# A hybrid streaming-encoder block on one core: the experts' gather of token rows is issued one block further ahead

## The chip, the cores and the metric

One core of one Trainium2 chip runs the whole layer in one launch. The metric is the device time of the program in microseconds; the median of several runs is compared.

## What is computed

The reference is one layer over 2048 tokens of width 1024: a mixing part (sparse attention and an mLSTM, each projected, gated and added to the residual), and then a mixture of experts. Only the experts matter here:

```
y = zeros(t, dm)
buf_tok, block_e = tokens sorted by expert, each expert padded to whole blocks of 128
xb = xn[buf_tok].reshape(nblk, 128, 1024)
def expert_block(xblk, e):
    hid = silu(xblk @ w_gate[e]) * (xblk @ w_up[e])      # 1024 -> 512, twice
    return hid @ w_down[e]                                # 512 -> 1024
y[buf_tok] += expert_block(...) * gate weight
```

There are 32 experts, each token goes to two of them, and the reference works in float32. With these inputs the padded list has 48 blocks of 128 rows; the table has room for 63.

## The kernel before

The stages follow one another: norm and input projection, indexer and top-k, attention and mLSTM, output projection with the router, and last `route_and_experts`, which the change touches. That function first sorts the tokens: it makes a table of row indices `IX` (one column of 128 indices for each block), the expert of each block `BE`, and the number of blocks in use, `used` (48 here). Then it runs the blocks, and last it combines: for each tile of tokens the two rows of results are gathered and added to the residual.

Float32 products are made as three products of rounded halves: each weight tile and each activation tile is split into a high part (a cast on ScalarE) and a low part (a subtraction on VectorE). A block `n` goes through these steps, each engine with its own program and semaphores between them:

- SyncE's queue loads the weights of a block into `raw`, one buffer deep: 8 pairs of gate and up tiles (`load_gate_up`, lines 575 and 576, 256 KB each) as soon as the low part of the tile that was there is made, then 4 down tiles (`load_down`, line 583, 512 KB each). A load whose expert is the one already there is skipped.
- GpSimd gathers the block's 128 token rows of 4 KB (`gather`, line 638) into one half of the tile `XG`, from a column of indices that it copies first (`indices`, line 641). The same engine stores each block's result (`store`, line 648) after ScalarE and VectorE have copied it out of PSUM into `Y`, each one half (lines 786 and 923).
- TensorE transposes the rows (`rows_t`, line 700, into `e_pX`), multiplies by gate and up (`gate_up`, line 710, 48 matmuls into `e_pG`), transposes the hidden values (line 717, `e_pH`) and multiplies by down (`down`, line 728, 24 matmuls into `e_pY`).
- ScalarE makes the high parts (`e_x_hi` line 761, `e_h_hi` 778, weights 768 and 781) and the Silu (773); VectorE makes the low parts (901, 915, weights 906 and 918) and the product of gate and up (911).

TensorE is software-pipelined. Its turn `n` of the loop is: transpose the hidden values of block n-1, gate and up of block n, the rows of block n+1, down of block n-1. So the transposes of block n+1 stand behind the gate-and-up matmuls of block n. GpSimd's turn `n` waits until gather n has landed (`x_in`) and until the rows of block n-1 are transposed (`xt_ps`), which frees the half of `XG` that gather n+1 writes; it copies the indices of block n+1, gathers block n+1, and then waits for the result of block n-1 and stores it. Each engine's program is run in order, and there is one store and one gather in each turn. A gather also sits in the same software queue of DMAs as the stores.

The final gather of the loop is one past the last block in use (its rows are transposed, but no product uses them).

Of the kernel before, what the change touches and what calls it, by code (L numbers as in the profile page):

```python
# [11 lines left out]
I32 = mybir.dt.int32  # L12
# [5 lines left out]
P = 128  # L18
# [22 lines left out]
NBLK = 63  # L41
# [64 lines left out]
def hold(eng, held):  # L106

    eng.sem_inc(held, 1)


def identity(nc, pool, tile, sem):

    nc.gpsimd.memset(tile, 0.0).then_inc(sem, 1)
    pool.wait_ge(sem, 1)
    nc.gpsimd.affine_select(out=tile, in_=tile, compare_op=ALU.not_equal, fill=1.0, base=0,
                            pattern=[[-1, P]], channel_multiplier=1).then_inc(sem, 1)
# [374 lines left out]
def route_and_experts(pg, LG, BI):  # L491
# [5 lines left out]
    with ExitStack() as c:  # L497
        sb = lambda n, s, d=F32: c.enter_context(nc.sbuf_tensor("e_" + n, s, d))
        sem = pg.semaphores(c, "e_", "y_ps ya_ok yv_ok")
        raw = sb("raw", [P, NU, 1024])  # L500
        w_hi, w_lo = sb("w_hi", [P, NU, 1024], F32R), sb("w_lo", [P, NU, 1024], F32R)
        IX, IXF = sb("ix", [P, NBLK + 1], I32), sb("ix_f", [P, NBLK])
        XG, ix = sb("xg", [P, 2, DM]), sb("ix_now", [P, 2], I32)
        x_hi, x_lo = sb("x_hi", [P, KT, P], F32R), sb("x_lo", [P, KT, P], F32R)
        SG, H = sb("sg", [P, DE]), sb("h", [P, DE])
# [51 lines left out]
        x_in, y_st = pg.sw_sem("e_x_in"), pg.sw_sem("e_y_st", primed=True)  # L557
# [3 lines left out]
        def blocks_in_use(eng):  # L561

            eng.wait_ge(be_ok, 1)
            return (eng.value_load(BE[0:1, USED:USED + 1], min_val=2 * NT, max_val=NBLK),
                    eng.value_load(BE[0:1, LAST:LAST + 1], min_val=2 * NT - 1, max_val=NBLK - 1))
# [51 lines left out]
        @block.gpsimd  # L617
        def _(pool):
            g = nc.gpsimd
            g.iota(w4i[:, 0, :], [[-1, NG]], base=NG, channel_multiplier=0)  # L620
            g.iota(w8i[:, 0, :], [[-1, EG]], base=EG, channel_multiplier=0)
            g.iota(ti[:, :, :], [[0, 2], [1, NT]], base=0, channel_multiplier=0)
            g.iota(pi[:, :], [[0, 1]], base=0, channel_multiplier=1)
            g.iota(ci[:, :], [[1, P]], base=0, channel_multiplier=0).then_inc(r_set, 1)
            g.memset(ones[:, :], 1.0)
            g.memset(IX[:, NBLK:NBLK + 1], 0)
            g.memset(lt[:, :], 1.0).then_inc(r_set, 1)
            pool.wait_ge(r_set, 2)
            g.affine_select(out=lt[:, :], in_=lt[:, :], compare_op=ALU.is_gt, fill=0.0, base=0,
                            pattern=[[1, P]], channel_multiplier=-1).then_inc(r_set, 1)  # L630
            identity(nc, pool, IDN[:, :], setup)
            g.memset(Z[:, :], 0.0).then_inc(setup, 1)
            pool.wait_ge(hot_ok, 1)
            g.tensor_tensor(in_blk[:, :, 1, :], hot, tf[:, :, :].broadcast_to([P, 2 * NT, NBLK]), ALU.mult).then_inc(blk_ok, 1)
            used, end = blocks_in_use(pool)

            def gather(n, b):
                pool.indirect_dma_start(XG[:, b, :], None, pg.d["xn"], bass.IndirectOffsetOnAxis(ix[:, b:b + 1].bitcast(U32), 0)).then_inc(x_in, 16)

            def indices(n, b):  # L640
                nc.gpsimd.tensor_copy(ix[:, b:b + 1], IX[:, bass.ds(n, 1)]).then_inc(ix_ok, 1)  # L641
                pool.wait_ge(ix_ok, n + 1)
                hold(pool, held)

            def store(n):
                pool.wait_ge(ya_ok, n + 1 + START)
                pool.wait_ge(yv_ok, n + 1 + START)
                pool.dma_start(yb_d[bass.ds(n * P, P), :], Y[:, :]).then_inc(y_st, 16)
            pool.wait_ge(tab_ok, 1)
            indices(0, 0)  # L650
            gather(0, 0)
            indices(1, 1)
            pool.wait_ge(x_in, 16)
            gather(1, 1)
            with pool.Fori(0, NBLK // 2) as t:
                for b in range(2):
                    n = 2 * t + b + 1
                    with pool.If(n < used):
                        pool.wait_ge(x_in, 16 * n + 16)
                        pool.wait_ge(xt_ps, n)  # L660
                        indices(n + 1, b)
                        gather(n + 1, b)
                        store(n - 1)
            store(end)
            pool.wait_ge(x_in, 16 * used + 16)
            pool.wait_ge(y_st, 16 * used + PRIMED)
            hold(pool, held)
            pool.wait_ge(gl, KT * used + KT)
            hold(pool, held)
            for t in range(NT):  # L670
                if t >= YBUF:
                    pool.wait_ge(c_ok, t - YBUF + 1)
                for k in range(2):
                    pool.indirect_dma_start(YG[t % YBUF][:, k, :], None, yb_d, bass.IndirectOffsetOnAxis(SL[:, k, t:t + 1].bitcast(U32), 0)  # L674
                                            ).then_inc(g_in[t % YBUF], 16)
# [1755 lines left out]
def build(nc, ins, out):  # L2431
    pg = Prog(nc, ins)
    pg.out = out
    with ExitStack() as c:
        h_hi = c.enter_context(nc.sbuf_tensor("h_hi", [P, KT, SEQ], F32R))
        h_lo = c.enter_context(nc.sbuf_tensor("h_lo", [P, KT, SEQ], F32R))
        project_head(pg, h_hi, h_lo)
        tail_and_index(pg, h_hi, h_lo)
    attend_and_recur(pg)
    with ExitStack() as c:  # L2440
        LG, BI = c.enter_context(nc.sbuf_tensor("logits", [P, NT, NG + NE], F32)), c.enter_context(nc.sbuf_tensor("router_bias", [P, 1, NG + NE], F32))
        merge_and_output(pg, LG, BI)
        route_and_experts(pg, LG, BI)
# [15 lines left out]
```

## Time and profile before

| | |
|---|---|
| median of 3 runs | 3496.93 us (3492.85 to 3497.88) |
| the profiled execution's own time | 3494.54 us |
| its span | 3492.5 us |
| TensorE busy | 3015.0 us (86% of the span) |
| VectorE busy | 2485.5 us (71%) |
| ScalarE busy | 1836.7 us (53%) |
| GpSimd busy | 449.1 us (13%) |
| mean granted TensorE clock | 0.936 |
| DMA, mean over the span | 154 GB/s |

The busy times are shares of the whole span, over stages with different limits. What bounds the expert stage is read from that stage: from the order of the instructions on each engine, with the idle time before each and what ended it. In the rows below PE is TensorE, PEld its weight loads, DVE VectorE, ACT ScalarE, POOL GpSimd, SPq the DMA queue of SyncE. `e_xg` is the tile XG, `e_ix_now` the copied indices, `slot_out` the results in memory. L with a number is a line of the kernel.

### The profile page before, as it was taken

What the parts mean: (1) busy time and instruction counts of PE and PEld (TensorE: products, weight loads), DVE (VectorE), ACT (ScalarE), POOL (GpSimd) and SP (SyncE); (2) the same over time, 40 slices, a digit from 0 to 9 for tenths busy, and PEclk for the clock granted to TensorE, in tenths of its full rate; (3) what the DMA queues carried; (4) which work ended last, traced back from release to release, by engine and by line L of the source; (5) the groups of instructions that cost most, each with busy time, mean ns of one, the idle gap of its engine ahead of it and who ended that gap; (6) DMA issues with size and microseconds to landing.
All of it is one profiled execution on the core that took longest, in us unless ns stands there. A gap on an engine that the chain in (4) does not pass through costs nothing. (4 is left out here: it accounts for less than half of the span.)

```text
span 3492.5 us, 45322 instructions
## 1 busy us (share of the span) xinstructions
PE 3015.0 (86%) x12983; PEld 2239.0 (64%) x12984; DVE 2485.5 (71%) x3902; ACT 1836.7 (53%) x2533; POOL 449.1 (13%) x587
## 2 busy tenths in 40 slices
PE   2898599889999967999999589998599999999980
PEld 2676477668778834555545367786477777777760
DVE  4457689889989966776663344442899989898874
ACT  6232257568578633434434233332477777777760
POOL 0111100000000032221111000000111111111113
PEclk6999799999999978999999789998699999999995
DMA  3122322222212265444323455553479779666868
GB/s 108 57 76 67 101 78 77 67 70 73 77 59 74 70 150 139 114 106 116 93 59 68 127 181 167 165 175 107 159 270 338 284 285 350 246 224 255 309 267 342
DMA packets 367694, 536.98 MB, mean 154 GB/s; under 512 B 35632, under 2 KB 201040, under 8 KB 367424
## 3 DMA queue, kind: packets, MB, share of 16 engines
q1 hardware_dynamic: 338288, 430.70, 39.0%
q0 software_dynamic: 26960, 96.13, 7.4%
q10 hardware_dynamic: 2304, 8.39, 0.6%
q8 instruction: 72, 1.18, 0.1%
q14 instruction: 70, 0.57, 0.1%
HBM read 510.18 MB, written 129.80 MB: 183 GB/s over the span
## 5 line engine op out<-in xcount | busy, mean ns | idle before, releaser
L906 DVE TENSOR_TENSOR e_w_lo<-e_raw,e_w_hi 128x1024 fp32r<-128x1024 f32 x386 | 446.9, 1218 | 3.3 <-ACT e_w_hi L768 3.3
L1539 PE MATMUL x_ps<-h_hi,x_w_hi 128*128 128x512 f32 (+1 forms) x1024 | 402.2, 393 | 0.0
L1539 PE MATMUL x_ps<-h_lo,x_w_hi 128*128 128x512 f32 (+1 forms) x1024 | 400.9, 391 | 0.0
L1539 PE MATMUL x_ps<-h_hi,x_w_lo 128*128 128x512 f32 (+1 forms) x1024 | 400.5, 391 | 0.0
L768 ACT CAST e_w_hi<-e_raw 128x1024 fp32r<-128x1024 f32 x386 | 376.8, 1051 | 5.3 <-PE e_pG L710 5.3
L1729 DVE TENSOR_SCALAR_CACHE_REDUCE x_relu<-x_score,x_cand 128x1024 uint8<-128x1024 f32 (+3 forms) x217 | 315.6, 1487 | 3.6
L1642 ACT ACTIVATE x_relu<-x_score,x_cand 128x896 int8<-128x896 f32 (+3 forms) x217 | 281.0, 1296 | 55.8 <-DVE x_cand L1736 55.5
L2297 DVE CUSTOM_DVE_ANT_0 t_junk<-t_L,t_mask 128x512 bf16<-128x512 f32 (+3 forms) x320 | 185.7, 607 | 164.6 <-PE t_L L2079 163.6
L2118 PE MATMUL t_O<-t_probT,t_v 128*65 128x512 f32 x544 | 289.6, 614 | 11.8 <-ACT t_probT L2269 10.5
L2269 ACT ACTIVATE t_probT<-t_ST 128x512 f32<-128x512 f32 x272 | 160.8, 593 | 260.3 <-PE t_ST L2110 259.6
L710 PE MATMUL e_pG<-e_w_hi,e_x_hi 128*128 128x512 f32 x768 | 247.0, 402 | 3.6 <-DVE e_x_lo L901 3.6
L710 PE MATMUL e_pG<-e_w_hi,e_x_lo 128*128 128x512 f32 x768 | 242.8, 397 | 0.0
L710 PE MATMUL e_pG<-e_w_lo,e_x_hi 128*128 128x512 f32 x768 | 242.8, 397 | 0.0
L2079 PE MATMUL t_L<-t_k,t_q 128*128 128x512 f32 (+3 forms) x320 | 194.8, 658 | 43.2 <-DVE t_max_part L2297 24.8
L918 DVE TENSOR_TENSOR e_w_lo<-e_raw,e_w_hi 128x1024 fp32r<-128x1024 f32 x192 | 222.3, 1220 | 11.8 <-ACT e_w_hi L781 11.8
L1539 PEld LDWEIGHTS x_ps<-h_hi,x_w_lo 128*128 128x128 f32 (+1 forms) x1024 | 191.2, 187 | 43.2
L1539 PEld LDWEIGHTS x_ps<-h_hi,x_w_hi 128*128 128x128 f32 (+1 forms) x1024 | 191.2, 187 | 42.4
L1539 PEld LDWEIGHTS x_ps<-h_lo,x_w_hi 128*128 128x128 f32 (+1 forms) x1024 | 191.3, 187 | 40.4
L781 ACT CAST e_w_hi<-e_raw 128x1024 fp32r<-128x1024 f32 x192 | 187.1, 1057 | 0.0
L1696 DVE SCALAR_TENSOR_TENSOR x_score<-x_relu,x_iw,x_score 128x1024 f32<-128x1024 f32 (+7 forms) x154 | 152.8, 1022 | 31.3 <-ACT x_relu L1616 26.9
L1616 ACT ACTIVATE x_relu<-x_z 128x1024 f32<-128x1024 f32 (+7 forms) x176 | 139.0, 817 | 67.2 <-DVE x_score L1696 43.9
L710 PEld LDWEIGHTS e_pG<-e_w_lo,e_x_hi 128*128 128x128 f32 x768 | 145.1, 189 | 35.0
(402 smaller groups left out, 6242.9 us busy)
## 6 DMA issues: line engine op xcount, KB each, us to landing
e_raw<-in_w_exp_gate SPq DMA_DIRECT2D x392, 256.0 KB
e_raw<-in_w_exp_up SPq DMA_DIRECT2D x392, 256.0 KB
e_raw<-in_w_exp_down SPq DMA_DIRECT2D x192, 512.0 KB
projT<-x_out SPq DMA_DIRECT2D x124, 256.0 KB
slot_out<-e_y POOLq DMA_DIRECT2D x48, 512.0 KB, 6.1
o_gate<-projT SPq DMA_DIRECT2D x32, 512.0 KB
x_w_raw<-in_w_in SPq DMA_DIRECT2D x31, 512.0 KB
x_t<-in_x SPq DMA_DIRECT2D x16, 512.0 KB
```

What stands on the lines that cost most here:

```text
L710: last = nc.tensor.matmul(psG[:, q, :], x[:, k, :], w[:, k, q * DE:(q + 1) * DE], start=(k == 0 and r == 0), stop=(k == KT - 1 and r == 2))
L768: nc.scalar.copy(w_hi[:, u, :], raw[:, u, :]).then_inc(gh, 1)
L781: nc.scalar.copy(w_hi[:, KT + k, :], raw[:, KT + k, :]).then_inc(dh, 1)
L906: nc.vector.tensor_tensor(w_lo[:, u, :], raw[:, u, :], w_hi[:, u, :].bitcast(F32), ALU.subtract).then_inc(gl, 1)
L918: nc.vector.tensor_tensor(w_lo[:, KT + k, :], raw[:, KT + k, :], w_hi[:, KT + k, :].bitcast(F32), ALU.subtract).then_inc(dl, 1)
L1539: last = nc.tensor.matmul(ps[0:w, u % 4, :], wt[:, m % 2, kk, 0:w], ht[:, kk, q * 512:(q + 1) * 512], start=(kk == 0 and s == 0), stop=(kk ...
L1642: nc.scalar.activation(unused[j][:, 0:width(n)], S[:, j, 0:width(n)], ACT.Sign, bias=cand[:, j:j + 1].bitcast(F32), accum_out=cnt[:, j:j + ...
L1729: last = v.tensor_scalar(unused[j][:, 0:width(n)], S[:, j, 0:width(n)], cand[:, j:j + 1].bitcast(F32), 0.0, ALU.is_ge, ALU.add, accum_out= ...
L2079: nc.tensor.matmul(L[:, made % 3, 0:hi - lo], Q[:, n % 4, h, :], KS[:, v, lo:hi], start=True, stop=True).then_inc(l_ok, 1)
L2118: nc.tensor.matmul(O[0:AD + 1, :, :], V[:, j, v, :], PT[:, (FIRST[s] + j) % 3, :], start=(j == 0), stop=(j == n)).then_inc(pv_ok, 1)
L2269: a.activation(PT[:, f % 3, :], ST[:, u % 2, :], ACT.Exp).then_inc(p_ok, 1)
L2297: v_.tensor_tensor_reduce(junk[:, seen % 3, 0:hi - lo], L[:, seen % 3, 0:hi - lo], MB[:, n % 4, lo:hi], 1.0, -3e38, ALU.add, ALU.max, mxp[ ...
```

## The change

The index table gets one more column, set to zero like the one before it. Before the loop GpSimd now issues the gather of block 2 as well, after gather 1 has landed and block 0 has been transposed. Turn `n` of the loop then waits for gather n+1 and for the transposes of block n, and gathers block n+2 into the other half of XG, ahead of the store of block n-1. The last wait counts one gather more.

```diff
-        IX, IXF = sb("ix", [P, NBLK + 1], I32), sb("ix_f", [P, NBLK])
+        IX, IXF = sb("ix", [P, NBLK + 2], I32), sb("ix_f", [P, NBLK])
...
-            g.memset(IX[:, NBLK:NBLK + 1], 0)
+            g.memset(IX[:, NBLK:NBLK + 2], 0)
...
             indices(1, 1)
             pool.wait_ge(x_in, 16)
             gather(1, 1)
+            pool.wait_ge(x_in, 32)
+            pool.wait_ge(xt_ps, 1)
+            indices(2, 0)
+            gather(2, 0)
             with pool.Fori(0, NBLK // 2) as t:
                 for b in range(2):
                     n = 2 * t + b + 1
                     with pool.If(n < used):
-                        pool.wait_ge(x_in, 16 * n + 16)
-                        pool.wait_ge(xt_ps, n)
-                        indices(n + 1, b)
-                        gather(n + 1, b)
+                        pool.wait_ge(x_in, 16 * n + 32)
+                        pool.wait_ge(xt_ps, n + 1)
+                        indices(n + 2, 1 - b)
+                        gather(n + 2, 1 - b)
                         store(n - 1)
             store(end)
-            pool.wait_ge(x_in, 16 * used + 16)
+            pool.wait_ge(x_in, 16 * used + 32)
```

## Rows read from the trace of the kernel before

**Rows 1.** The page's 40 slices of the span: TensorE's granted clock in tenths.
```profile
PEclk6999799999999978999999789998699999999995
```

**Rows 2.** View by window, first store to last but one: us, busy, clock, DMA share, GB/s.
```profile
2528.82:3390.65 861.83, 837.76 (x3855) 674.16 (x3853) 776.06 (x736) 645.87 (x735) 134.58 (x139) 1.00 0.76 282
```

**Rows 3.** Order of time on POOL: start us, us, instruction, idle before it and releaser.
```profile
2528.82 0.59 POOL L648 DMA_DIRECT2D slot_out<-e_y  x1 [34.60 <-DVE e_y L923]
...
2604.50 0.58 POOL L648 DMA_DIRECT2D slot_out<-e_y  x1 [15.94 <-DVE e_y L923]
2605.08 1.21 POOL L641 COPY e_ix_now<-e_ix 128x1 int32 x1
2607.08 1.16 POOL L638 DMA_INDIRECT e_xg<-xn,e_ix_now  x1 [0.79 <-POOL e_ix_now L641]
2622.60 0.58 POOL L648 DMA_DIRECT2D slot_out<-e_y  x1 [14.36 <-DVE e_y L923]
...
2642.18 0.58 POOL L648 DMA_DIRECT2D slot_out<-e_y  x1 [15.83 <-DVE e_y L923]
...
3390.65 0.58 POOL L648 DMA_DIRECT2D slot_out<-e_y  x1 [16.15 <-DVE e_y L923]
```

**Rows 4.** Order of time on PE, around the transposes of two blocks.
```profile
2614.39 1.04 PE L700 MATMUL e_pX<-e_ident,e_xg 128*128 128x128 f32 x8
...
2632.03 0.63 PE L710 MATMUL e_pG<-e_w_hi,e_x_lo 128*128 128x512 f32 x2
2633.90 1.09 PE L700 MATMUL e_pX<-e_ident,e_xg 128*128 128x128 f32 x8 [1.24 <-DMA e_xg<-xn,e_ix_now]
```

**Rows 5.** Chain of waits, same stretch: start us, us, what.
```profile
2625.18 8.68 DMA e_xg<-xn,e_ix_now
```

**Rows 6.** Waits from 2528.82 to 3390.65: us in total, times, longest.
```profile
PE e_pX L700 <- DMA e_xg<-xn,e_ix_now: 21.8, 24, 1.6
PEld e_pX L700 <- DMA e_xg<-xn,e_ix_now: 36.1, 31, 2.0
SPq L108 <- DVE e_w_lo L918: 183.9, 184, 3.6
```

**Rows 7.** The gathers of token rows, from issue to landing.
```profile
DMA to landing us min/median/max: 4.4/7.6/9.0
```

**Rows 8.** Order of time on POOL, PE, SP's queue and ACT at the first blocks.
```profile
2493.06 1.16 POOL L638 DMA_INDIRECT e_xg<-xn,e_ix_now  x1 [0.79 <-POOL e_ix_now L641]
2504.25 1.04 PE L700 MATMUL e_pX<-e_ident,e_xg 128*128 128x128 f32 x8
2510.70 0.38 SPq L576 DMA_DIRECT2D e_raw<-in_w_exp_up  x1
2516.57 1.05 ACT L768 CAST e_w_hi<-e_raw 128x1024 fp32r<-128x1024 f32 x1 [0.28 <-PE e_pG L710]
```

**Rows 9.** View by window, the two of 50 us with the highest DMA share.
```profile
2650.00:2700.00 50.00, 49.53 (x231) 39.92 (x230) 45.38 (x44) 36.97 (x44) 7.58 (x9) 1.00 0.98 367
2900.00:2950.00 50.00, 49.78 (x228) 39.64 (x227) 45.17 (x44) 38.73 (x45) 8.76 (x9) 1.00 1.04 399
```

**Rows 10.** DVE: one copy of a result (order of time), and all waits before it.
```profile
2621.17 0.69 DVE L923 COPY e_y<-e_pY 128x512 f32<-128x512 f32 x1 [0.70 <-PE e_pY L728]
DVE e_y L923 <- PE e_pY L728: 43.6, 46, 1.1
```

**Rows 11.** Loads on SP's queue, the cast behind them, and landings of 512 KB there.
```profile
2613.16 0.08 SPq L575 DMA_DIRECT2D e_raw<-in_w_exp_gate  x1
2650.82 0.35 SPq L575 DMA_DIRECT2D e_raw<-in_w_exp_gate  x1
2663.50 5.79 ACT L768 CAST e_w_hi<-e_raw 128x1024 fp32r<-128x1024 f32 x6
DMA to landing us min/median/max: 5.5/8.3/10.5
```

**Rows 12.** Chain of waits: the gate-and-up matmuls of block 0 and of block 8.
```profile
2491.15 13.26 PE e_pG L710 x48
2641.04 11.19 PE e_pG L710 x48
```

## The prediction

> **What bounds the kernel now.** I read the page first. The change touches only the expert stage, which runs from about 2477 us to 3411 us; TensorE's clock stands at its full level there except at the two ends [rows 1]. A view by window from the first store of a block to the store of the last block but one says how tight it is [rows 2]: 861.83 us, PE busy 837.76 of them, VectorE 776.06, ScalarE 645.87, the DMA engines at 0.76. TensorE sets the pace, and what it lacks is some 24 us. Next I read GpSimd's order of time [rows 3]. Each block shows a store, a copy of indices and a gather, and the distance between two stores is the period of a block: 18.10 us from 2604.50 to 2622.60, 19.58 from there to 2642.18. From the first store to the last one listed are 46 periods. I counted them in that view: 15 are 18.09 to 18.12 us and 31 are longer (18.33 to 19.88). Then TensorE's order of time [rows 4]: in the short period the transposes of a block's token rows (e_pX) follow the gate-and-up matmuls without a gap; in the long one they start at 2633.90, though the matmuls before them were issued to the end by 2632.5. The chain of waits gives the reason [rows 5]: the gather issued at 2625.18 lands 8.68 us later, at 2633.86, and the transposes start 0.04 us after that. The waits of the stretch say the same in sum [rows 6]: PE and its weight loads wait before e_pX for the gather and for nothing else. Both lines see the same gaps, so they are not added.
>
> The arithmetic of one gather: it is issued 2.58 us behind the store (2607.08 against 2604.50), which waits for the result of the block two before. The transposes want it at 2614.39, 7.31 us after its issue. Gathers take 4.4 to 9.0 us to land, 7.6 in the median [rows 7]. So about a third are in time and the rest cost up to 1.8 us.
>
> **The change, part by part.** The loop does the same three things in the same order, but the gather in it is for block n+2 instead of n+1. In time each slot still holds a store and, 2.58 us behind it, a gather; only whose rows it fetches is new.
> - *The gather's lead.* A slot's gather is now wanted one period later: 7.31 + 18.10 = 25.4 us after its issue, against 9.0 at the longest. No transposes should wait. All 46 periods become 18.10: 46 x 18.10 = 832.6 us instead of 861.83, **29.2 us less**. (Summed over the 31 long periods alone the excess over 18.10 is also 29.2.)
> - *Its new waits.* It waits for the gather before it (issued 18.1 us earlier, landed within 9.0) and for the transposes of block n, which frees its half of XG. In the old order of time the transposes at 2614.39 stand ahead of the store at 2622.60, behind which the new gather comes. Both are met when POOL gets there. Cost 0. Queued behind the gather is the store of block n-1, for whose result POOL waits some 14.4 us after the gather anyway. If a wait did hold POOL, it would have to do so for that long before Y, and with it the copies of the next result, came late.
> - *POOL's and the queues' load.* Per block the same copy (1.2 us), the same gather, the same store. One more gather in all, of a block past the last, and one column more set to zero long before: 0. SP's queue is not passed by anything.
> - *The start.* The gather of block 2 goes out as before, at 2493.06; the gather of block 3 moves from 2531 to some 2 us after the transposes of block 1, so to about 2507.3 [rows 8]. That falls among the loads of block 2's gate and up weights, whose last is issued at 2510.70. It adds 512 KB; at the 399 GB/s that the busiest window moved [rows 9] that is 1.3 us. ScalarE casts the late ones from 2516.57 on, waiting for PE then, and the matmuls that read them come only after the result of block 0, behind 2527. I take 0 and keep 0 to 1.3 us.
> - *What is late next.* With the gather gone, VectorE: in the short period it still waits 0.70 us for the result of the down matmuls before it copies it [rows 10], and it does that in every one of the 46. Its start is set by PE each time, so short periods in a row don't eat that margin. SP waits 183.9 us for VectorE in its queue, 4 us per block, so it isn't the bound either [rows 6]. ScalarE waits for PE alone.
> - *The weights' cover.* In a block with a new expert SP issues the first load at 2650.82 and ScalarE casts it at 2663.50, 12.7 us later. Loads of 512 KB on that queue landed in 5.5 to 10.5 us [rows 11]. That leaves 2.2 us at the worst and 4.4 in the median.
>
> Sum: 3494.54 (the profiled execution's own time) - 29.2 = 3465.3. That execution is 2.4 us under the median of the three runs, 3496.93, so the median should be **3467.7 us**.
>
> At one place a rule of the Trainium skill speaks against the change. Its page "DMA: Bandwidth & Descriptors", section "Anatomy of one DMA — SWDGE (gpsimd) path", has a DMA issued from GpSimd take 2.0 us plus its bytes at 436 GB/s; for the 512 KB of a gather that is an estimate of 3.2 us. By it every gather would be in time already, and the sum would be 0. The measured landings [rows 7] are all longer, so the rule gets no term here.
>
> **The rivals.**
> *A, the gather is not what the transposes lack, no change.* A wait is put down to the semaphore that came last, so the name could be wrong, and a gather could always be in time, as by the skill's rule above. It would give 3497. Against it: 0.04 us between landing and start, and gaps only where the landing is beyond 7.3 us. Chance 0.04.
> *B, the DMA engines hold part of the gain.* Where several experts in a row are new, the DMA engines are full: 399 GB/s at a share of 1.04 in one window of 50 us, 367 at 0.98 in another [rows 9]. Such a block moves 16 loads of 256 KB and 4 of 512 KB of weights, a gather and a store of 512 KB each, in all 7 x 1024 KB = 7.34 MB; at 399 GB/s that is 18.4 us, and the periods there are 18.33 to 18.47. If that bound them and not the gather, they would keep 0.35 us each. SP's own times tell the blocks with new weights from the others, 0.34 us for a load that runs and 0.08 for one that is skipped [rows 11]; the longest row of them is 5 blocks, so weights fall behind by 1.7 us at most, inside the cover of 2.2 to 4.4 us; hence I believe they will run at 18.1. If not, some 9 blocks keep 3.2 us (gain 26.0, 3471), and if all 31 blocks with new weights (32 experts) did, 10.9 us (gain 18.3, 3479). Chance 0.10.
> *C, slower: TensorE's clock.* Without its pauses TensorE is busy all the time, and the grant could fall from 2.4 to 1.2 GHz for stretches. Price: the gate-and-up matmuls of block 0, partly at the lower level, took 13.26 us, at the full level 11.19 [rows 12]; that is 2.07 us each time, so the gain is gone when it happens in more than 14 of the 46 blocks; in all 46 it would be 95 us lost, less 29 gained, 3563. Against it: the grant was at half where PE was idle and 1.00 over the whole stretch with PE at 97% [rows 2]. Chance 0.03.
>
> **The numbers.** The forecast has 0.83, B 0.10, A 0.04, C 0.03. The forecast's own range is 3463 to 3473 (the three runs lie 4 us below to 1 us above their median; the start may cost 1.3). With B's upper case the range is 3461 to 3478. A measurement of this kernel can tell about 0.2%, 7 us, from no change. Faster by more: forecast and B, 0.93. Within: A, 0.04. Slower: C, 0.03.
>
> **What would show it.** After the change GpSimd's stores should stand 18.1 us apart in all 46 periods, the waits before e_pX should be gone from PE and its loads, the gathers should land in the same 7 to 9 us, DMA_INDIRECT e_xg should count 50 instead of 49, and the same window should be 833 us with PE busy at 99% or more. B shows as periods of 18.4 with ScalarE waiting for a DMA before its casts, or VectorE's 0.70 us gone; A as unchanged gaps; C as a PEclk below 1.00 within the stretch. I am wrong if the stage shortens by less than 26 us.

## The result, and the profile after

The changed kernel takes 3463.52 us in the median of 4 runs (3459.86 to 3467.85) against 3497.40 us (3492.85 to 3499.34) for the kernel before, measured beside it: ratio 0.9904, 95% interval 0.9892 to 0.9917. The forecast was 3467.7 us in a range of 3461 to 3478.

The first view again by window, from the first store of a block to the store of the last block but one (us of stretch, busy time of PE, PE's loads, DVE, ACT, POOL, granted clock, DMA share, GB/s):

```profile
2530.37:3363.52 833.15, 831.58 (x3855) 677.20 (x3854) 773.91 (x736) 646.01 (x735) 132.81 (x138) 1.00 0.79 290
```

Against [rows 2] the stretch is 28.7 us shorter, with the same 3855 matmuls. PE is busy for all but 1.6 us of it, at the same full clock, and the DMA engines move about the same bytes in less time (282 GB/s over 861.83 us, 290 over 833.15). The order of time on POOL shows where the distance between two stores has gone (against [rows 3]; an edit shifts the line numbers, so L923 of the kernel before is L927 here, L700 is L704, L710 is L714 and L728 is L732):

```profile
2507.00 0.18 POOL L641 COPY e_ix_now<-e_ix 128x1 int32 x1 [10.94 <-PE e_pX L704]
2507.97 0.97 POOL L638 DMA_INDIRECT e_xg<-xn,e_ix_now  x1 [0.79 <-POOL e_ix_now L641]
2530.37 0.59 POOL L648 DMA_DIRECT2D slot_out<-e_y  x1 [21.43 <-DVE e_y L927]
...
2602.77 0.58 POOL L648 DMA_DIRECT2D slot_out<-e_y  x1 [14.38 <-DVE e_y L927]
2603.35 1.20 POOL L641 COPY e_ix_now<-e_ix 128x1 int32 x1
2605.34 1.16 POOL L638 DMA_INDIRECT e_xg<-xn,e_ix_now  x1 [0.79 <-POOL e_ix_now L641]
2620.89 0.58 POOL L648 DMA_DIRECT2D slot_out<-e_y  x1 [14.38 <-DVE e_y L927]
...
3363.52 0.58 POOL L648 DMA_DIRECT2D slot_out<-e_y  x1 [14.38 <-DVE e_y L927]
```

The gather still follows the store by 2.57 us, and 44 of the 46 periods are 18.07 to 18.13 us. The other two are 19.52 and 16.70 us, 36.22 together: one store was issued 1.4 us late, with no releaser that the profile names, and nothing behind it moved. GpSimd pauses so in the kernel before too, one turn of its loop later and ahead of a gather, which follows its store by 3.99 us instead of 2.58, in a block that had room for it (a period of 18.12 us). TensorE's order of time, at the block where it stood still before [rows 4], has no gap any more; the chain of waits of that stretch names PE alone:

```profile
2630.32 0.62 PE L714 MATMUL e_pG<-e_w_hi,e_x_lo 128*128 128x512 f32 x2
2630.78 1.03 PE L704 MATMUL e_pX<-e_ident,e_xg 128*128 128x128 f32 x8
2631.57 0.72 PE L732 MATMUL e_pY<-e_w_hi,e_h_hi 128*128 128x512 f32 x2
```

```profile
2613.70 5.61 PE e_pY L732 x24
2619.31 0.44 PE e_pH L721 x4
2619.74 11.19 PE e_pG L714 x48
2630.94 0.87 PE e_pX L704 x8
```

The landings of the gathers have not become shorter (against [rows 7]), and VectorE still waits in each of the 46 blocks for the down matmuls, 0.7 us (32.8 us in all, against [rows 10]). From the answers for the gather's line and from the waits of the stretch:

```profile
L638 POOL DMA_INDIRECT e_xg<-xn,e_ix_now x50: 967/1155/1165, 2481.3 to 3348.0; - x50
DMA to landing us min/median/max: 4.3/7.6/9.7
```

```profile
DVE e_y L927 <- PE e_pY L732: 32.8, 46, 0.7
```

The rest of the program is as it was: from the first gather's issue to the first store 49.04 us, before 48.90; from the last store of the stretch to the end of the span (3466.0 us) 102.48 us, before 101.85. The first gather itself came 1.4 us later in this execution, in stages that the change doesn't touch. So the two profiled executions differ by 26.5 us in span where the stage gives 28.7, and the medians by 33.9.

### The profile page after: what moved, and what is told of

It is laid out like the page before. It is cut to its first block and busy times, and to the rows that moved or that the text cites. A ratio compares the mean times of both kernels' runs of the same rounds, so it can differ in the third digit from the quotient of the medians.

```text
span 3466.0 us, 45327 instructions
## 1 busy us (share of the span) xinstructions
PE 3004.1 (87%) x12983; PEld 2238.1 (65%) x12984; DVE 2482.6 (72%) x3902; ACT 1836.6 (53%) x2533; POOL 447.2 (13%) x589
## 5 line engine op out<-in xcount | busy, mean ns | idle before, releaser
L714 PE MATMUL e_pG<-e_w_hi,e_x_hi 128*128 128x512 f32 x768 | 246.7, 402 | 3.6 <-DVE e_x_lo L905 3.6
L714 PE MATMUL e_pG<-e_w_lo,e_x_hi 128*128 128x512 f32 x768 | 242.6, 397 | 0.0
L714 PE MATMUL e_pG<-e_w_hi,e_x_lo 128*128 128x512 f32 x768 | 242.1, 396 | 0.0
L2083 PE MATMUL t_L<-t_k,t_q 128*128 128x512 f32 (+3 forms) x320 | 195.0, 658 | 44.1 <-DVE t_max_part L2301 26.5
L714 PEld LDWEIGHTS e_pG<-e_w_hi,e_x_lo 128*128 128x128 f32 x768 | 145.2, 189 | 35.1
```

The costliest lines, as they stand in the source:

```text
L714: last = nc.tensor.matmul(psG[:, q, :], x[:, k, :], w[:, k, q * DE:(q + 1) * DE], start=(k == 0 and r == 0), stop=(k == KT - 1 and r == 2))
L2083: nc.tensor.matmul(L[:, made % 3, 0:hi - lo], Q[:, n % 4, h, :], KS[:, v, lo:hi], start=True, stop=True).then_inc(l_ok, 1)
```

## The experiments

The theory was that only the time from a gather's issue to its use counts. The rivals were that the place in the program or the extra gather helps, that a whole block of lead is needed, that GpSimd's turn is near the path, and for the size, that there is a gain outside the stage. "The stage" below is always the stretch between the same two stores, read by window. The changed kernel, again:

> The changed kernel as it is, timed again in more rounds. The profile of after accounts for 28.7 us in the expert stage, the medians for 33.9 us. Theory (the gather's lead and nothing else): the gain settles at 27 to 31 us, ratio 0.9911 to 0.9923, and the stage from the first store to the last but one is 833 us in the profile again. Rival (the change also helps outside the stage): the gain stays at 33 to 35 us, ratio near 0.990.

It took 3464.88 us (4 runs, 3459.84 to 3469.33) beside 3495.81 us (15 runs, 3490.36 to 3500.09): 0.991, interval 0.9895 to 0.9926. The profile's stage was 833.15 us once more, to the hundredth. So the changed kernel's stage repeats; the kernel before was profiled once, 861.83 us, and the run that follows, which does the same work in the same order, has 862.84. What the medians show beyond 28.7 us (33.9, then 30.9 us) shrank in the second series and lies inside the spread of single runs: 8.0 and 9.5 us between the fastest and the slowest of the changed kernel in the two series, 6 to 18 us of the kernel before in the series measured. A gain outside the stage is not shown, and the interval doesn't exclude a few microseconds.

**The two halves of the change.**

```diff
-                        indices(n + 2, 1 - b)
-                        gather(n + 2, 1 - b)
                         store(n - 1)
+                        indices(n + 2, 1 - b)
+                        gather(n + 2, 1 - b)
```

> The changed kernel with the store of block n-1 put in front of the gather of block n+2 in the same turn. Theory (only the time between a gather's issue and its use counts, and gather n+2 behind store n-1 is what the kernel before does, written with another index): as before, 3494 to 3500 us, the stage 860 to 863 us, 30 or so long periods. Rival (being two blocks ahead in the program, with the extra gather before the loop, is what helps): as after, 3460 to 3468 us, the stage 833 us.

3494.85 us (10 runs), ratio 0.9999 (0.9987 to 1.0011), and by window:

```profile
2527.27:3390.11 862.84, 840.06 (x3855) 675.73 (x3853) 775.93 (x736) 646.16 (x735) 134.69 (x139) 1.00 0.76 282
```

The gain is gone in full. "One block further ahead" and "in front of the store" are one thing: with the store in front, the gather of n+2 waits for the result of n-1, as it did in the kernel before under another index.

**How much lead is needed.** In the kernel before, the index copy goes ahead of the store and the gather stays behind it (`hold` increments a semaphore; the index table also gets the second extra column, as in the change):

```diff
             gather(1, 1)
+            indices(2, 0)
...
                         pool.wait_ge(xt_ps, n)
-                        indices(n + 1, b)
+                        hold(pool, held)
                         gather(n + 1, b)
+                        indices(n + 2, 1 - b)
                         store(n - 1)
```

> The kernel before, gather still one block ahead and behind the store of the block before, but its indices are copied ahead of that store, so that the gather follows the store by 0.6 us instead of 2.58: some 1.9 us more lead, 9.2 us instead of 7.3. Theory (a gather that has landed is worth nothing more, so lead counts only up to the 9.0 us of the longest landing): nearly the whole gain, the stage 833 to 836 us, 3464 to 3471 us. Rival (a whole block of lead is needed, because landings stretch as the pace rises or the gather comes to lie closer behind the store's packets): landings grow to over 9.2 us, half or more of the stalls stay, 3475 to 3490 us.

3466.14 us (5 runs), ratio 0.9917 (0.9903 to 0.9931). The order of time on POOL, the stage by window, and the landings:

```profile
2600.75 0.58 POOL L648 DMA_DIRECT2D slot_out<-e_y  x1 [15.19 <-DVE e_y L925]
2601.72 1.62 POOL L638 DMA_INDIRECT e_xg<-xn,e_ix_now  x1 [0.40 <-issue]
2603.35 0.32 POOL L641 COPY e_ix_now<-e_ix 128x1 int32 x1
```

```profile
2528.35:3361.52 833.17, 831.59 (x3855) 677.12 (x3854) 773.90 (x736) 646.06 (x735) 109.53 (x138) 1.00 0.79 291
```

```profile
DMA to landing us min/median/max: 4.2/6.8/8.7
```

The gather follows the store by 0.97 to 1.26 us (2.39 once, at the pause), so 1.3 to 1.6 us sooner, not the 1.9 of the expectation, and this edit alone brings the whole gain: 833.17 us for the stage. A whole block of lead is not needed. In the changed kernel the longest landing is 9.7 us, 2.4 beyond the old lead of 7.31, so of the 18.1 us that the change adds not more than 2.4 are used.

The edit does two things, though, and the run doesn't part them: it gives lead, and it puts the gather 0.9 to 1.2 us ahead of the down loads on SP's queue, where it was 0.4 us behind them (the groups of blocks in this paragraph are told apart below, by what SP's queue loads). The landings moved both ways. In a group of 16 blocks they were 7.7 to 9.0 us and are now 6.4 to 6.9. The other 30 became longer: 15 were 7.4 to 8.2 us and are 7.9 to 8.7, and 15 were 4.7 to 5.5 us and are 5.6 to 7.1. So the rival was right that landings stretch, for 30 of the 46, and wrong in size: against a lead of some 8.6 to 8.9 us, TensorE waited once, for 0.2 us. The longest landings have next to nothing to spare.

The other way round, both kernels with the indices copied twice, which moves each gather back (in the order of time of the kernel before so edited it follows the store by 3.70 to 3.71 us, 2611 to 2671 us into the span, and by 2.58 without the edit, so by 1.13 us more and not the 2.0 of the expectations, since the second copy takes 0.97 us):

```diff
-                nc.gpsimd.tensor_copy(ix[:, b:b + 1], IX[:, bass.ds(n, 1)]).then_inc(ix_ok, 1)
-                pool.wait_ge(ix_ok, n + 1)
-                hold(pool, held)
+                for again in range(2):
+                    nc.gpsimd.tensor_copy(ix[:, b:b + 1], IX[:, bass.ds(n, 1)]).then_inc(ix_ok, 1)
+                    pool.wait_ge(ix_ok, 2 * n + again + 1)
+                    hold(pool, held)
```

> The changed kernel with the indices copied twice, so that each gather is issued about 2.0 us later. Theory: the lead falls from 25.4 to 23.4 us against landings of at most 9.7 us, no change: 3460 to 3468 us, the stage 833 us, no wait before the transposes. Rival (POOL's turn is itself near the path, so that its store or the copies behind it come late): up to 46 x 2.0 us more, over 3475 us.

The changed kernel doesn't notice: the stage 833.15 us, no wait before the transposes. Its median, 3468.48 us (4 runs, 3465.21 to 3470.20), is 0.5 us above the range expected and 3.6 above the 3464.88 us of its partner; the single runs of the two overlap, and the stage has none of it.

> The kernel before with the indices copied twice, so that each gather is issued about 2.0 us later: the lead falls from 7.3 to 5.3 us. Theory (each period is 18.10 plus what the landing takes beyond the lead): the 31 long periods grow by 2.0 us each and the 15 short ones by something under 2.0, in all 62 to 92 us: the stage 924 to 954 us, 3559 to 3589 us. Rival (the stalls are not the gather's): under 20 us more.

The kernel before does: 3531.86 us (2 runs), ratio 1.0113 (1.0083 to 1.0142), the stage 896.11 us, 34.3 more. That is half of what was expected, and in sum what the theory gives for the delay that the edit really made: 31 long periods by 1.13 us are 35.0. It holds in the sum only: single long periods changed by -0.4 to 3.8 us, since the landings moved as well, so the close agreement is in part luck. The short periods stayed short (14 of 15; one turned long, 18.70 us, at the pause of GpSimd), so those gathers had over 1.1 us to spare. The waits of the stretch:

```profile
PEld e_pX L701 <- DMA e_xg<-xn,e_ix_now: 65.9, 32, 2.8
PE e_pX L701 <- DMA e_xg<-xn,e_ix_now: 51.9, 32, 2.3
```

Two kinds of gather, then: some 30 that are late, and 15 that have room. That set the next question.

**What makes a gather late.** The kernels from here to the one with the narrow store and no loads leave out part of the stores or use wrong weights, so their results are wrong; each was executed once, and only the stage and the landings are read. First the store ahead of the gather in its queue against the loads of weights:

```diff
-                pool.dma_start(yb_d[bass.ds(n * P, P), :], Y[:, :]).then_inc(y_st, 16)
+                pool.dma_start(yb_d[bass.ds(n * P, P), 0:16], Y[:, 0:16]).then_inc(y_st, 16)
```

> The kernel before with a store of 16 of the 1024 columns in the loop (64 bytes a row instead of 4 KB); the other columns of the results are filled with zeros after the loop, so only the expert stage is to be read, and the end is longer. Theory T1 (a gather lands late because the store issued 2.58 us ahead of it fills the same software queue): landings fall by 1.3 us or more, to a median of 6.3 us or less, and the stage comes to 833 to 838 us. Theory T2 (the landing is set by the weights' loads on the other queue, or is simply what 128 rows of 4 KB take from GpSimd): the median stays at 7.3 us or more, the stage above 850 us.

The stage got longer, 870.06 us against 861.83, and the landings with it, 8.0 us in the median:

```profile
DMA to landing us min/median/max: 4.3/8.0/9.3
```

T1 fell. Why a store of 8 KB in place of 512 KB makes the gather behind it later is taken up below. Then no loads, by making all entries of the table of experts 0:

```diff
-            v.tensor_scalar(BE[:, 0:NBLK], psH[0:1, 0, 0:NBLK], float(NE - 1), None, ALU.min)
-            v.memset(BE[:, NBLK:USED], NE - 1)
+            v.tensor_scalar(BE[:, 0:NBLK], psH[0:1, 0, 0:NBLK], 0.0, None, ALU.min)
+            v.memset(BE[:, NBLK:USED], 0)
```

> The kernel before with all blocks on expert 0, so that no weights are loaded in the loop (the results use the weights of expert 0 throughout); gathers and stores are the same. T1 (the store ahead of it in the queue makes the gather late): landings stay at 7 us or more and the stage above 850 us. T2 (the weights' loads make it late): landings fall below 7.3 us nearly everywhere and the stage comes to 833 to 840 us.

```profile
2524.17:3356.71 832.54, 830.97 (x3855) 676.65 (x3853) 773.85 (x736) 646.84 (x735) 134.50 (x138) 1.00 0.18 63
```

```profile
DMA to landing us min/median/max: 4.2/4.5/7.0
```

Without loads the gather of the kernel before is in time in every block, and 832.54 us is what TensorE needs: the changed kernel is 0.6 us above it. The loads make gathers late, but not all of them alike. SP's queue in the kernel before tells which; `load_down` is issued some 0.4 us ahead of the gather at 2607.08 or 2625.18 [rows 3]:

```profile
2586.98 3.66 SPq L583 DMA_DIRECT2D e_raw<-in_w_exp_down  x4
2606.66 3.40 SPq L583 DMA_DIRECT2D e_raw<-in_w_exp_down  x4
2624.76 3.67 SPq L583 DMA_DIRECT2D e_raw<-in_w_exp_down  x4
```

A group of 3.66 or 3.67 us is one whose loads ran, one of 3.40 was skipped (its last load takes 0.07 instead of 0.34 us). Set beside the 46 periods, all 31 long periods have loads that ran, with landings of 7.4 to 9.0 us, and all 15 short ones skipped ones, with landings of 4.7 to 5.5 us. One edit each for the two kinds of loads:

```diff
-                    load_down(this, dict(cond=this != before), n - 1)
+                    load_down(this, dict(cond=this != this), n - 1)
```

> The kernel before with the down weights never reloaded in the loop (all blocks multiply by the down weights of expert 0), gate and up loads as they were. Theory T3: a gather is late where the four down loads (2 MB) are issued 0.4 us ahead of it on the other queue, as every long period of the kernel before has a down load that runs and every short one a skipped one. Then landings fall to 7.3 us or less, the stage comes to 832 to 835 us. Rival T4 (any traffic of weights does it, mostly the gate and up loads with twice the bytes): the stage stays above 845 us.

```profile
2532.14:3364.68 832.54, 830.97 (x3855) 676.68 (x3853) 773.62 (x736) 645.71 (x735) 134.38 (x139) 1.00 0.60 214
```

```profile
DMA to landing us min/median/max: 4.3/5.3/7.3
```

```diff
-                    load_gate_up(after, dict(cond=after != this), n)
+                    load_gate_up(after, dict(cond=after != after), n)
```

> The kernel before with the gate and up weights never reloaded in the loop (all blocks multiply by those of the first two experts loaded), down loads as they were. T3 (the down loads make the gather late): the same 31 or so long periods, landings up to 8.5 us, the stage 850 to 862 us. T4 (the gate and up loads do): the stage 832 to 840 us.

```profile
2534.07:3401.33 867.26, 837.54 (x3855) 674.29 (x3853) 776.41 (x736) 645.84 (x735) 134.44 (x139) 1.00 0.37 135
```

```profile
DMA to landing us min/median/max: 4.3/8.0/9.4
```

T3 holds. A third of the bytes, the down loads, makes all of the stalls; two thirds, the gate and up loads, make none, though the DMA engines are at a share of 0.60 with them. What it is about the down loads was not parted: that they are issued 0.4 us ahead of the gather, that they are 512 KB each, or that their rows are 4 KB where those of gate and up are 2 KB.

What was not expected is that without the gate and up loads the stalls grow, to 867.26 us: 30 long periods, landings to 9.4 us. With the narrow store, that is two cases in which less traffic made the gather later. The trace of the kernel before has the same pattern in it. SP's queue issues the gate and up loads of the next block ahead of the down loads; in 15 of the 31 long periods they ran, in 16 they were skipped:

| | 16 blocks, gate and up skipped | 15 blocks, gate and up ran |
|---|---|---|
| landing of the gather, median | 8.6 us | 7.7 us |
| its range | 7.7 to 9.0 us | 7.4 to 8.2 us |
| the median without gate and up loads | 8.7 us | 8.2 us |
| sum of the periods, kernel before | 311.3 us | 279.0 us |
| the same periods, no gate and up loads | 309.9 us | 285.8 us |
| the same periods, narrow store | 314.3 us | 284.2 us |

So the gather lands latest where the down loads have no other weights ahead of them in their queue, and without gate and up loads only the 15 blocks that lost them grew, by 6.8 us. For that run this tells where the loss is. With the narrow store both groups grew, by 3.1 and 5.2 us, which the pattern explains at most in part. The pattern is a correlation in these traces; no run moved the down loads by themselves, and how the engines share their time between the two queues stays open.

Last the narrow store without loads:

> The kernel with the narrow store (16 of 1024 columns, the rest of the results set to zero after the loop) and with no loads of weights in the loop (all blocks on expert 0), so that a gather has the DMA engines to itself. With the full store ahead of it and no loads the median landing was 4.5 us. If the store ahead costs the gather nothing, it stays at 4.2 to 4.6 us; if the store's 512 KB come first in the queue, it falls by about the 1.3 us that they take, to 3.2 us or so. The stage 832.5 us either way.

The landings were these, with 1.8 us for the narrow store itself in place of 3.0 us for the full one:

```profile
DMA to landing us min/median/max: 4.3/4.5/7.2
```

So the store costs the gather nothing when both have the DMA engines to themselves; the stage was 832.5 us (2528.27 to 3360.81).

**Where the DMA engines are the bound.** Rival B of the prediction, made the rule: the weights of every block are loaded (`{}` in place of both conditions), in the changed kernel and in the one before.

> The changed kernel with the weights of every block loaded, also where the expert stays the same, so that each block moves 7.34 MB. It tests rival B of the prediction. At 399 GB/s a block takes 18.4 us of the DMA engines. Theory: in a row of 46 such blocks the weights fall behind by 0.3 us each until the cover of 2.2 to 4.4 us is used up, after 7 to 15 blocks, and then the DMA engines set the pace at 18.4 us: the stage 841 to 847 us, ScalarE waiting for loads before its casts. Rival (DMA has room beyond 399 GB/s, or the cover never ends): the stage stays at 833 us. A second rival (gathers and weights in competition land much later): over 850 us.

The stage was 847.25 us, the upper end of the theory's 841 to 847. The window, and what ScalarE waits for:

```profile
2525.21:3372.46 847.25, 840.58 (x3855) 677.30 (x3853) 773.64 (x736) 658.11 (x735) 102.77 (x138) 1.00 1.04 398
```

```profile
ACT e_w_hi L772 <- DMA e_raw<-in_w_exp_up: 166.0, 207, 2.3
```

The bound is real: 398 GB/s at a share of 1.04, and periods of 18.41 to 18.47 us nearly throughout, as the 18.4 worked out from 7.34 MB. But it took hold at the fourth period, not after 7 to 15, so that the cover of the weights is smaller than had been put, at least at the start of the stage, where ScalarE already waits 1.8 us for a load in the first period (at 2535.0). The exceptions among the periods, 19.83, 16.38 and 19.08, stand at GpSimd's pause.

> The kernel before with the weights of every block loaded, the partner of the changed kernel with the same edit, which took 847.25 us for the stage at 18.43 us a block. Theory (with the DMA engines as the bound, the gather's lead is worth nearly nothing): the stage 847 to 851 us, so that the change is worth 0 to 4 us there, in the medians 3484 to 3490 us. Rival (the gather's lateness adds to the DMA engines' bound, since the down loads are behind it in every block): 19 us or more a block, the stage over 870 us.

857.50 us, which is neither expectation. The waits of the stretch (2528.56 to 3386.06) say that the loads of weights, at 395 GB/s for all DMA, don't set the pace here: ScalarE waits for no load, and TensorE waits for the gather in every block:

```profile
PEld e_pX L700 <- DMA e_xg<-xn,e_ix_now: 33.5, 46, 2.9
```

So the two limits don't add; the one that ends last counts, by the waits the gather in each block, with periods of 18.25 to 19.27 us and one of 22.3 (POOL paused ahead of its gather there). The difference to the changed kernel is 10.3 us, 3.9 of them in that one period. And with more loads than in the kernel before, down loads in all 46 blocks instead of 31, the stage is 4.3 us shorter: gate and up loads ran ahead of all the down loads, and the landings in the stretch were 7.4 to 8.5 us, as in the right column above. In the whole times, taken in two series, the two can't be told apart: 3484.19 us (8 runs, ratio to the kernel before 0.9969, 0.9952 to 0.9986) for the changed one, 3489.72 us (5 runs, 0.9960, 0.9932 to 0.9989) for the other.

## Why the prediction was right, point by point

- *The bound and the stall.* TensorE sets the pace of the stage and a late gather is all that it waited for. Shown from both ends: lead added (early indices, the change) or the loads removed beside which gathers are late (no loads, no down loads) each gives 832.5 to 833.2 us. One reading is off by little: the matmuls before the late transposes ended at 2632.66 by [rows 4], not by 2632.5.
- *The lead.* 46 periods of 18.10 us were forecast, 832.6 us, and 833.15 measured: a gain of 28.7 us for 29.2. The difference is 0.01 us a period. The sum against the profiled execution's own time gave 3465.3 us, and 3467.85 was measured there, of which 1.4 us are a later start of the stage.
- *The new waits and POOL's turn: 0.* Right; 1.1 us of further delay in POOL's turn changed nothing in the stage. POOL's store, once 1.4 us late, moved nothing either.
- *The start: 0 to 1.3 us.* It was 0.14 us.
- *VectorE next.* Its margin stayed at 0.7 us in every block, as forecast.
- *The weights' cover.* The conclusion was right for this kernel: all blocks with new experts run at 18.1 us, ScalarE waits for no load in the stretch, and rival B was false here. The periods of 18.33 to 18.47 us on which it rested were late gathers of 7.4 to 7.6 us. The cover itself was overestimated; the run with all loads used it up 3 blocks behind the first store. Two readings were too kind. The 12.7 us are those of the first of eight pairs of loads; the up tile of the sixth is issued at 2657.42 and cast at 2668.24, 10.8 us later. And the landings of 5.5 to 10.5 us [rows 11] are of eight loads of `x`, issued from 2494.0 to 2497.7, not of weights. With longer rows of new experts the step would have failed, as the run with all loads shows.
- *Rival A* fell with the gain itself, with the chain of waits and with the early indices. *Rival C*: the granted clock stayed at 1.00 with PE at 99.8%. The estimate of 3.2 us for 512 KB from the fit of the Trainium skill ("DMA: Bandwidth & Descriptors", section "Anatomy of one DMA — SWDGE (gpsimd) path") is short even of a gather without any loads beside it, 4.5 us in the median; a store of 512 KB without loads took 3.0 us, close to it.
- *The median* is 4.2 us below the forecast. No step of the sum accounts for it; the second series brought 3464.88 us, and single runs of either kernel lie 6 to 18 us apart. That the median fell inside the range is thus no finer proof than the spread allows; the mechanism rests on the stage. The lower end of the range, 3461, isn't worked out in the prediction, whose own figures lead to 3463; the median, 3463.52, lies above both.

What the prediction missed was the cause behind the landings. It took 7.6 us as what a gather takes, with a spread. It is 4.5 us alone, 4.7 to 5.5 where the down loads are skipped, and 7.4 to 9.0 where 2 MB of down weights are issued 0.4 us ahead of it. That didn't matter for the sum, because the new lead covers both; but it would have shown a second way to the same gain, and why the 15 short periods are short.

## What to carry to other kernels

Measure a prefetch by its lead: from issue to first use, against the longest landing. If the lead is just short, ask first what stands between the moment when the transfer could go and when it does: here 1.3 to 1.6 us, won by copying the indices earlier (which also put the gather ahead of the down loads), were worth as much as a whole block ahead, but left next to no margin, where the whole block leaves more than 15 us. A transfer's landing time isn't a property of the transfer alone: set the late ones beside what other queues issue in the same microsecond, for one kind of neighbour may cause nearly all of it. Two late things need not add: in the kernel before with all loads both the DMA engines and the gather were short of time, and only the later of the two counted in a block. And moving an operation across another in a software pipeline may be the same as changing its index; the run with the store in front showed the two to be one change.

## What the runs showed that was not expected

- Less traffic made the gather later: with the store cut from 512 KB to 8 KB the median landing went from 7.6 to 8.0 us and the stage from 861.83 to 870.06 us; without gate and up loads to 8.0 us and 867.26 us. For the second the traces show in which blocks the loss is, those where gate and up loads had run ahead of the down loads; the mechanism was not tested.
- The copy of 128 indices takes 1.1 to 1.2 us behind the store, where VectorE runs subtractions that read two SBUF tiles, 0.32 us where it starts later in such a subtraction (early indices), and 0.18 us at 2507.00 in the changed kernel, where VectorE runs none of them but the product of gate and up, whose one input is in PSUM. In the kernel before each of the 49 copies ends 0.04 to 0.05 us after the subtraction that was under way when it began, wherever in it it began. The Trainium skill ("SBUF — State Buffer", section "Who interferes with whom") says that a VectorE instruction with two SBUF inputs contends with a GpSimd instruction that reads SBUF, and that the port pair they share is an exclusive lock; these rows agree, and no run was made for it.
